# A decoder trunk's key/value stage, attention opening and output projection, with transfers and small steps in another order

## What is computed

```python
kv_new = (x @ attn_w_kv).reshape(b, n, N_DIL_GROUPS, 2, HEADS_PER_GROUP, HEAD_DIM)
...
x = layer_norm(ALPHA * x + 0.5 * swiglu(x, ffn_w13[layer, 0], ffn_w2[layer, 0]), ln_g[layer, 0], ln_b[layer, 0])
...
    mix = dilated_mixer(x, kv_groups, q_offs, attn_w_q[j], attn_w_o[j], rel_bias)
x = layer_norm(ALPHA * x + mix, ln_g[layer, 1], ln_b[layer, 1])
x = layer_norm(ALPHA * x + 0.5 * swiglu(x, ffn_w13[layer, 1], ffn_w2[layer, 1]), ln_g[layer, 2], ln_b[layer, 2])
```

## Time and profile before

| what | value |
|---|---|
| median of 3 runs | 2139.33 us (2139.27 to 2141.32) |
| profiled execution, its own time | 2139.55 us |
| its span in the trace | 2137.8 us |
| mean granted clock of TensorE | 0.982 of full speed |
| busy, share of the span | TensorE 97%, VectorE 66%, ScalarE 41%, POOL 11% |
| chain that ended last, by engine | PE 76%, DVE 11%, DMA 5%, ACT 3%, issue 3% |

### The profile page before, as it was taken

The page is one execution under the profiler, slowest core; times in us unless marked ns, Lnnn a source line. Parts: engine busy times, 40 slices in busy tenths (PEclk is TensorE's granted clock), DMA queues, the critical chain, the costliest instruction groups (busy, mean ns, idle before and its releaser), DMA issues.

```text
span 2137.8 us, 43528 instructions
## 1 busy us (share of the span) xinstructions
PE 2068.2 (97%) x16575; PEld 2005.9 (94%) x16575; DVE 1421.5 (66%) x2358; ACT 867.4 (41%) x1529; POOL 239.9 (11%) x283
## 2 busy tenths in 40 slices
PE   7999999999999999999999999999979989999998
PEld 7999999999999999999999999998976789999997
DVE  4583895594895598389649936257737578838955
ACT  3351454362553255255325524322225545424533
POOL 0000002304000000410000031101105230000022
PEclk8999999999999999999999999999989999999998
DMA  4332433222233233324433333567669423323331
GB/s 145 89 116 87 128 116 108 77 70 83 79 99 102 87 99 100 88 81 138 121 91 99 101 92 96 177 212 240 195 217 296 142 71 99 113 74 100 98 95 56
DMA packets 381761, 249.87 MB, mean 117 GB/s; under 512 B 10678, under 2 KB 363294, under 8 KB 381582
## 3 DMA queue, kind: packets, MB, share of 16 engines
q1 hardware_dynamic: 371271, 210.00, 33.1%
q0 software_dynamic: 10352, 37.95, 5.2%
HBM read 230.63 MB, written 22.35 MB: 118 GB/s over the span
## 4 chain that ended last, share of the span: by engine, by line
PE 76%; DVE 11%; DMA 5%; ACT 3%; issue 3%; SPq 1%; POOL 1%; DVEq 0%; ACTq 0%; POOLq 0%
PE pair L796 33%; PE pair L928 30%; PE pair L835 5%; DMA t_w_raw<-in_attn_w_kv 2%; PE pair L1076 2%; DVE t_w_sum L2042 1%; DVE t_w_seven L2047 1%; PE pair L808 1%; DVE t_w_lo L1925 1%; DVE t_u_sum L2330 1%; DMA t_w_raw<-in_ffn_w 1%; DMA t_cached_v<-in_cache_kv_w 1%; PE pair L1325 1%; DVE t_x_diff_lo L2019 1%; DVE t_stream L2255 1%
## 5 line engine op out<-in xcount | busy, mean ns | idle before, releaser
L928 PE MATMUL pair<-t_x_diff_hi,t_w_seven 128*128 128x272 f32 x1960 | 409.9, 289 | 0.0
L1459 ACT ACTIVATE t_w_hi<-t_w_raw 128x1024 fp32r<-128x1024 f32 (+2 forms) x140 | 163.8, 1172 | 413.9 <-PE pair L796 344.4
L928 PEld LDWEIGHTS pair<-t_x_diff_hi,t_w_seven 128*128 128x128 f32 x1960 | 320.4, 188 | 0.0
L1925 DVE TENSOR_TENSOR t_w_lo<-t_w_raw,t_w_hi 128x1024 fp32r<-128x1024 f32 (+2 forms) x140 | 216.2, 1544 | 155.1 <-ACT t_w_hi L1459 149.5
L928 PE MATMUL pair<-t_x_hi,t_w_seven 128*128 128x272 f32 x1120 | 240.1, 294 | 5.7 <-DVE t_c L2051 4.1
L928 PE MATMUL pair<-t_x_diff_lo,t_w_seven 128*128 128x272 f32 x840 | 241.6, 288 | 0.0
L796 PE MATMUL pair<-t_h_lo,t_w_hi 128*128 128x272 f32 x1144 | 236.5, 288 | 0.0
L796 PE MATMUL pair<-t_h_hi,t_w_lo 128*128 128x272 f32 x1144 | 236.5, 288 | 0.0
L796 PE MATMUL pair<-t_h_hi,t_w_hi 128*128 128x272 f32 x1144 | 236.3, 288 | 0.0
L928 PEld LDWEIGHTS pair<-t_x_hi,t_w_seven 128*128 128x128 f32 x1120 | 184.3, 188 | 16.2 <-issue 11.5
L796 PEld LDWEIGHTS pair<-t_h_hi,t_w_lo 128*128 128x128 f32 x1144 | 179.4, 188 | 0.0
(11 more groups left out here) (332 smaller groups left out, 5213.0 us busy)
## 6 DMA issues: line engine op xcount, KB each, us to landing
t_w_raw<-in_ffn_w SPq DMA_DIRECT2D x280, 256.0 KB, 3.1
t_w_raw<-in_ffn_w SPq DMA_DIRECT2D x64, 704.0 KB, 4.6
t_w_raw<-in_ffn_w SPq DMA_DIRECT2D x36, 512.0 KB, 3.8
t_cached<-in_cache_kv_w POOLq DMA_DIRECT2D x16, 1024.0 KB, 9.1
t_cached_v<-in_cache_kv_w POOLq DMA_DIRECT2D x32, 512.0 KB, 7.2
t_w_raw<-in_attn_w_kv SPq DMA_DIRECT2D x24, 512.0 KB, 6.8
t_w_raw<-in_attn_w_q SPq DMA_DIRECT2D x12, 512.0 KB, 3.9
scratch_bias_rows<-scratch_bias_row SPq DMA_DIRECT2D x12, 384.0 KB
```

The lines of the kernel that those rows point to most:

```text
L928: m = nc.tensor.matmul(out[:, 0:HALF], w[:, k, :], b, start=start and k == 0 and j == 0, stop=k == 3 and j == 2, skip_group_check=not start)
L1459: nc.scalar.activation(whi[s][:, 0:KT[stage], :], raw[s][:, 0:KT[stage], :], ACT.Copy) \
L1925: nc.vector.tensor_tensor(lo[:, 0:k, :], raw[s][:, 0:k, :], hi[:, 0:k, :].bitcast(F32), ALU.subtract).then_inc(lo_made[s], 1)
```

## The change

Six things are done, in five places.

1. In the `kv` stage, SP loads the first half of the next unit's weights ahead of two of the stores; the second half stays behind them.
2. Behind that stage, SP's order is: first half of `b0`, tokens of unit 10, second half of `b0`, tokens of unit 11, `b12`, the samples' stores, the prompt's values. The first tile of values has a semaphore of its own, `v0_in`.
3. POOL's loads of the cached values wait for `v0_in` alone.
4. TensorE computes the second pair of prompt scores ahead of the samples' new values, VectorE does the first pair's softmax step ahead of the copies of their result, and ScalarE turns the last tokens behind two copies for the samples' softmax. The buffers `s_prompt0` and `a_stat` lie elsewhere for this.
5. In `wo`, VectorE makes the sums instead of POOL, the first as copies; TensorE's last additions to them come at the first feature chunk of the second column half, no longer at the third and fourth.
6. The first unit of `up3a` has weight buffers of its own, rounded ahead of the means and the variance.

```diff
+def ahead(stage, i):
+    return stage == "up3a" and isinstance(i, int) and i == 0
...
-            for i in range(UNITS["kv"]):
-                stream("kv", i)
-                if i >= 1:
-                    kt_store(i - 1, 0)
-                    if i >= 2:
-                        kv_store(i - 2, 1)
-                    kt_store(i - 1, 1)
-                    kv_store(i - 1, 0)
+            stream("kv", 0)
+            stream("kv", 1)
+            for i in range(1, UNITS["kv"]):
+                kt_store(i - 1, 0)
+                if i >= 2:
+                    kv_store(i - 2, 1)
+                if i + 1 < UNITS["kv"]:
+                    stream("kv", i + 1, (0,))
+                kt_store(i - 1, 1)
+                kv_store(i - 1, 0)
+                if i + 1 < UNITS["kv"]:
+                    stream("kv", i + 1, (1,))
...
             bias0(0, 0, True)
+            kv_store(UNITS["kv"] - 2, 1)
             bias0(0, 1, True)
-            kv_store(UNITS["kv"] - 2, 1)
             kv_store(UNITS["kv"] - 1, 0)
             kv_store(UNITS["kv"] - 1, 1)
-            for g in range(NG):
-                sp.dma_start(O[f"kv_s{g}"].rearrange("b t k h d -> (b t) (k h d)"),
-                             kv_n[:, g * 2 * GW:(g + 1) * 2 * GW]).then_inc(kvn_out, 16)
...
+            for g in range(NG):
+                sp.dma_start(O[f"kv_s{g}"].rearrange("b t k h d -> (b t) (k h d)"),
+                             kv_n[:, g * 2 * GW:(g + 1) * 2 * GW]).then_inc(kvn_out, 16)
             for s in range(2):
                 sp.wait_ge(kv_out[s], 32 * UNITS["kv"])
-            load(v_p[0][:], kv0_d.ap().rearrange("(c p) n -> p c n", p=P)[:, :, GW:2 * GW], v_in)
+            load(v_p[0][:], kv0_d.ap().rearrange("(c p) n -> p c n", p=P)[:, :, GW:2 * GW], v0_in)
...
                             if j == 1 and s == 0 and k == 0:
                                 sums_early(stage, 0)
-                            if j == 1 and s == 0 and k == (1 if KT[stage] > 4 else 2):
+                            if j == 1 and s == 0 and k == (1 if KT[stage] > 4 else 0):
                                 sums_last(stage, 0)
-                            if j == 1 and s == 0 and k == 3:
+                            if j == 1 and s == 0 and k == (3 if KT[stage] > 4 else 0):
                                 sums_last_square(stage, 0)
...
             m.then_inc(pkey_t, 1)
+            scores(0, 1)
...
                         if first:
-                            pe.wait_ge(v_in, 16 * NG)
+                            pe.wait_ge(v0_in, 16)
+                            pe.wait_ge(v_in, 16 * (NG - 1))
...
+                if ahead(stage, i):
+                    act.wait_ge(o_ready, GC)
+                    nc.scalar.activation(whi3[s][:], raw[s][:, 0:DC, :], ACT.Copy).then_inc(hi_made[s], 1)
+                    return
...
+                if stage == "wo":
+                    round_hi(AFTER[stage], 0, 0)
                 means(0)
                 deviations(0)
-                round_hi(AFTER[stage], 0, 0)
+                if stage != "wo":
+                    round_hi(AFTER[stage], 0, 0)
...
-            kv_tokens(1, 11)
             act.wait_ge(snk_mm, 1)
             nc.scalar.activation(s_nk[:, 0:512], pb[0:SAMP, 0, :], ACT.Copy).then_inc(snk_ok, 1)
             nc.scalar.activation(s_nk[:, 512:768], pb[0:SAMP, 1, 0:256], ACT.Copy).then_inc(snk_ok, 1)
+            kv_tokens(1, 11)
...
             exps(0, 0)
+            act.wait_ge(kvn_out, 16 * NG)
...
+            def wo_sums(i, s):
+                n = ABASE["wo"] + 4 * i + 2 * s
+                first = first_turn(i) and s == 0
+                dve.wait_ge(res_made, RBASE["wo"] + 2 * i + s + 1)
+                if first:
+                    nc.vector.tensor_copy(accs[:], x[:, 0, :]).then_inc(acc_made, 1)
+                else:
+                    dve.wait_ge(acc_made, n - 1)
+                    nc.vector.tensor_tensor(accs[:], accs[:], x[:, 2 * i + s, :], ALU.add).then_inc(acc_made, 1)
+                dve.wait_ge(sq_made, RBASE["wo"] + 2 * i + s + 1)
+                if first:
+                    nc.vector.tensor_copy(accq[:], sq[:]).then_inc(acc_made, 1)
+                else:
+                    dve.wait_ge(acc_made, n)
+                    nc.vector.tensor_tensor(accq[:], accq[:], sq[:], ALU.add).then_inc(acc_made, 1)
...
                         round_lo(nxt, s, j)
+                        if stage == "wo":
+                            wo_sums(i, s)
...
+                if stage == "wo":
+                    round_lo(AFTER[stage], 0, 0)
                 variance(0)
                 deviation(0)
                 scaled(0, 0)
                 scaled(1, 0)
-                round_lo(AFTER[stage], 0, 0)
+                if stage != "wo":
+                    round_lo(AFTER[stage], 0, 0)
...
+            dve.wait_ge(b12_in, 32)
+            pair_scores(0, 0)
+            dve.wait_ge(snv_done, 1)
...
             dve.wait_ge(kvn_out, 16 * NG)
-            dve.wait_ge(b12_in, 32)
             for r in range(QB):
                 for c in range(GC):
-                    pair_scores(r, c)
+                    if r or c:
+                        pair_scores(r, c)
...
-            pool.wait_ge(v_in, 16 * NG)
+            pool.wait_ge(v0_in, 16)
...
             pool.wait_ge(o_ready, GC)
-            sums("wo")
             centre("wo")
```

42 lines of the change are left out of this document (26 added, 16 removed).

## The result

The changed kernel takes 2117.18 us (median of 4 runs, 2115.59 to 2122.55) against 2139.30 (4 runs, 2137.30 to 2141.32); the ratio is 0.9893, with a 95% interval of 0.9875 to 0.9912. (The interval of the ratio, applied to 2139.30, is 2112.6 to 2120.5 and reaches into the range.) The profiled execution takes 2118.12.

What follows compares the result with a forecast made beforehand. TensorE is busy in 97% of the span, so only its waits and low-clock stretches can be won. Key/value 9.2, opening 4.7 and projection 3.0 sum to 16.9, from 2139.55 to 2122.6 us; range 2117.9 to 2130.5.

Steps and rivals of the forecast that it cites:

- the second part, the gates: Opening: POOL's cached-value loads start 8.1 us earlier, 3.4 us of late tiles share the bus, so gain 4.7.
- The late bias, costed at nothing: Opening: issued behind the sample stores, it lands near 1591, covered by TensorE's work on the samples; cost nothing.
- The key/value term: Key/value stage: earlier weight load brings all six stalled turns to 17.03 us; gain 9.2, bounds 6.2 and 10.0.
- The clock there was a consequence: Key/value stage: clock of 0.97 over the six turns follows from the waits; the other 3 us of the gain.
- The projection: Output projection and norm: sums on VectorE and an advanced weight rounding gain 3.0 us, bounds 1.2 and 3.6.
- its half turn fits: Output projection: VectorE's half turn with the added sums takes 2.85 us against a period of 3.03, fitting by 0.2.
- the wait before the norm's units: Output projection's end: as a sign of being right, TensorE's wait of 4.22 us falls to about 1.2 to 2.
- A: Key/value stage: the stall is only handed on, to the load's second part or the keys; 2131.8 us, chance 0.08.
- B: Opening: cached values crowd out the prompt's values; 2124.2 us, at the far end 2135.1; chance 0.14.
- The share of 0.37: Opening: SP's share of the bus beside POOL's loads, by which the late tiles land by 1605.8, before the 1608.7 limit.
- C: Whole kernel: no change, loads move in the program but land as before; 2139.5 us, chance 0.04.
- D: Key/value stage: slower, SP's new wait becomes the pace of the stage; 2151.9 us, chance 0.02.

Runs made afterwards that it cites:

- gate_three: The changed kernel, but POOL's loads of the cached values wait for all three tiles of the prompt's values again; 2123.63 us.
- kv_only: The kernel before with only the key/value stage's first-half weight load moved ahead of the two stores; 2128.51 us, ratio 0.9946.
- no_gate: The changed kernel, but POOL's loads of the cached values wait for none of the prompt's value tiles; 2128.66 us.
- open_old: The changed kernel with the whole opening undone (SP's order, POOL's gate, order on three engines), key/value stage and output projection still changed; 2125.10 us.

## Why the prediction was wrong, and where it was right

**The step that failed** is in the second part, the gates: "3.4 us of transfer, 1.4 MB, shares the bus", by which POOL's lead of 8.1 became 4.7 at the landing. The lead was smaller, 6.6, since the first tile landed later than worked out, but all of it arrived: the last cached values came 7.0 earlier (44.6 to 37.6 us behind the stage's end). The bus I had seen full, 407 GB/s, was full of the prompt's values; POOL's own loads had not filled it. The windows of the kernel before behind POOL's start at 1603.56 (columns as above):

```profile
1604.00:1614.00 10.00, 9.71 (x134) 7.53 (x136) 9.66 (x25) 6.48 (x15) 9.94 (x24) 0.71 0.87 283
1614.00:1626.00 12.00, 8.71 (x134) 5.94 (x122) 7.33 (x18) 5.18 (x13) 3.65 (x11) 1.00 1.06 313
```

In these first ten us, while POOL issues twelve loads one after another, 0.55 to 0.74 us each, 283 GB/s move at a share of 0.87; after the change it is 371 at 1.03 in the ten us up to 1596 (above). So there was room at the start: 88 GB/s over ten us are 0.9 of the 1.4 MB. Taken from POOL's first issue on, much of the room is the time before the first bytes come:

```profile
1603.56:1604.56 1.00, 0.80 (x7) 0.83 (x8) 0.96 (x2) 0.00 (x0) 1.00 (x2) 0.50 0.00 0
1604.56:1605.56 1.00, 1.00 (x23) 0.71 (x22) 0.97 (x6) 0.46 (x1) 1.00 (x3) 0.50 0.59 209
1605.56:1613.56 8.00, 7.71 (x104) 5.91 (x88) 7.82 (x20) 5.58 (x13) 7.94 (x19) 0.74 0.96 309
```

The bus stands empty for a microsecond and is at 0.59 in the next, some 1.4 us with nothing to move; gate_three shows the same, 0.00 and 0.65. The gate on three tiles leaves this hole behind the tiles; the gate on one lets the late tiles fill it. (Where an expectation speaks of 209 GB/s, its window counts 1.6 us ahead of POOL's first load, and makes the room look larger than it was.) At 371 to 407 GB/s the hole is 0.5 to 0.6 MB. Whether POOL's issue holds the rate down behind it, 309 GB/s at a share of 0.96, is not shown; gate_three shows the consequence, that the tiles beside the start are free. What covers the rest of the 1.4 MB stays open.

**Left out and put at nothing.** The term left out is the clock behind the wait. The kernel before waits 1.92 for the second half of the cached values; its windows behind that wait:

```profile
1626.00:1628.00 2.00, 2.00 (x16) 0.48 (x15) 0.00 (x0) 0.51 (x2) 0.00 (x0) 0.72 0.99 341
1628.00:1630.00 2.00, 2.00 (x38) 1.47 (x34) 0.00 (x0) 0.00 (x0) 1.09 (x2) 0.50 1.03 387
1630.00:1632.00 2.00, 2.00 (x35) 1.64 (x34) 0.77 (x2) 0.20 (x1) 2.00 (x6) 0.93 0.95 305
```

The 16 products there take 2.73 us, and 1.92 in the changed kernel. From this point to the output projection it is 70.2 us before and 68.7 after: 1.5 that stand in no term of the sum. With 6.4 up to this point they make the 7.9. The late bias, costed at nothing with the condition that it is there near 1591, 9.8 behind the stage's end, came 11.0 behind it: VectorE stood 2.31 us before it, and TensorE 0.87 before the second scores.

**The rest of the miss**, 5.4 between 2122.6 and the median: 3.2 in the opening, 0.3 and 0.4 in the two other terms, 0.9 ahead of everything that the change touches, -0.3 behind it, and 0.9 between the profiled execution and the median. Without the opening's 3.2 the time would have lain in the range. So would it without the two 0.9, which are scatter and no gain of the change: that the median fell below the range, and not just inside, is chance.

**Right.** The key/value term to 0.3, with its mechanism, shown alone. The clock there was a consequence: it is 1.00 in all turns now. The projection to 0.4; its half turn fits, 0.41 to 0.88 us are left in each, so no wait for VectorE's adds appeared. Its parts were sized less well than their sum, 2.3 and 0.7 in place of 1.0 and about 2, and the wait before the norm's units is 2.62, above the 1.2 to 2 given as a sign; that the sum came out is in part luck. In the changed kernel's trace the engines, not the transfers, end the opening, as the cached values come in 0.8 before they are used: the forecast had it the other way.

**Rivals.** A fell with kv_only. B did not happen in the changed kernel, whose tiles land at 1591.1, 7.1 ahead of their use; no_gate shows that it was real, and that the gate on the first tile avoids it. The share of 0.37 that I took from the key/value stage was not seen: the last tile landed 4.4 us behind POOL's start, just as the sum has it without any sharing (1595.5 to 1599.9). C and D fell with the turns of 17.0.

## What to carry to other kernels

Before a load is charged for the bus that another takes, look at the GB/s of the very stretch, not at the highest one nearby, and at the time between the issue of the first load and its first bytes: here 1.4 MB beside twelve loads cost them nothing. A wait of TensorE can cost more than its length. Of the seven waits of 1.6 us or more for cached values in these traces, five were followed by the low clock (16 products in 2.73 to 3.64 us), but two were not: open_old waits 2.51, longer than the kernel before with its 1.92, and goes on at full speed.

```profile
1614.55 1.92 PE L1342 MATMUL pair<-t_cached_v,t_work 128*32 128x512 f32 x16 [2.51 <-DMA t_cached_v<-in_cache_kv_w]
```

So a forecast that removes a wait should read from the trace what the same instructions lose behind that very wait. Where a transfer is moved earlier, gate it on the first part of the more urgent one: no gate cost 11.5 us here, the full gate 6.4.

## What the runs showed unexpected

The first turn starts between 1404.8 and 1414.2 us in the fourteen traces, though the code up to there is the same in all; TensorE's waits for the start's loads and for the sums `t_c` differ, 7.9 and 1.4 in the earliest, 8.7 and 4.1 in the latest. That is a part of it only. The opening, too, differs among the three traces in which its code is the same (107.0, 110.0, 106.4), and in one of them TensorE waits 1.16 and 1.60 for cached values, in the others not at all. So differences under some 3 us in the opening are not told apart by one trace, nor under 4 by a few runs.
